# Feed-forward loop: two of eight gate and up tile pairs as 2x2 blocks in seven products

## What is computed

```python
h2 = rms_norm(x, norm2_w[l]) * (1.0 + sc2) + sh2
ff = (jax.nn.silu(h2 @ w_ffn_gate[l]) * (h2 @ w_ffn_up[l])) @ w_ffn_down[l]
x = x + g2 * ff
return rms_norm(x, final_w)
```

## Time and profile before

| | |
|---|---|
| median of three runs | 2235.95 us |
| the profiled execution, first to last instruction | 2234.2 us |
| TensorE busy | 2219.6 us, 99% of the span |
| VectorE / ScalarE / GpSimd busy | 1623.4 / 1104.2 / 136.7 us |
| granted TensorE clock, mean over the span | 0.999 |
| share of TensorE in the chain of work that ended last | 98% |
| HBM traffic | 244 GB/s over the span |

### The profile page before, as it was taken

How to read it: one execution, slowest core, us unless ns; L and a number is a source line. 1 busy time by engine, 2 the same in 40 slices (tenths; PEclk the granted TensorE clock), 3 DMA queues, 4 the chain that set the end, 5 groups by cost and what they waited for, 6 DMA issues and landing times.

```text
span 2234.2 us, 31225 instructions
## 1 busy us (share of the span) xinstructions
PE 2219.6 (99%) x10287; PEld 1848.7 (83%) x10287; DVE 1623.4 (73%) x2120; ACT 1104.2 (49%) x1437; POOL 136.7 (6%) x259
## 2 busy tenths in 40 slices
PE   9999999999999999999999999999999999999998
PEld 7888888888888888888888888888888888888886
DVE  5767778878875875887788877766665666666576
ACT  6455445666664344534366654444444443344444
POOL 1100110000000000010011110000000000000000
PEclk9999999999999999999999999999999999999999
DMA  8978897666665766697689987766766777777664
GB/s 304 339 237 300 314 337 242 208 209 208 214 232 182 288 229 205 211 338 269 197 299 317 325 294 251 243 208 214 235 221 232 238 241 229 237 230 226 209 218 147
DMA packets 157899, 551.78 MB, mean 247 GB/s; under 512 B 19441, under 2 KB 25328, under 8 KB 156288
## 3 DMA queue, kind: packets, MB, share of 16 engines
q1 hardware_dynamic: 112416, 405.92, 53.5%
q0 software_dynamic: 34304, 129.64, 17.0%
q10 hardware_dynamic: 11104, 15.22, 2.0%
HBM read 534.92 MB, written 10.53 MB: 244 GB/s over the span
## 4 chain that ended last, share of the span: by engine, by line
PE 98%; DVE 1%; DMA 1%; ACT 0%; issue 0%; DVEq 0%; ACTq 0%; SPq 0%
PE ps L2090 23%; PE ps L2092 23%; PE ps L2091 23%; PE ps L2208 7%; PE ps L2210 7%; PE ps L2209 7%; PE ps L2129 2%; PE ps L2338 1%; PE ps L2105 1%; PE ps L2107 1%; PE ps L2106 1%; PE ps L2268 0%; PE ps L2333 0%; PE ps L2528 0%; DMA raw<-ws_dram 0%; PE ps L2270 0%
## 5 line engine op out<-in xcount | busy, mean ns | idle before, releaser
L1195 DVE TENSOR_TENSOR w_lo<-raw,w_hi 128x1024 fp32r<-128x1024 f32 x757 | 921.4, 1224 | 512.8 <-ACT w_hi L675 499.1
L675 ACT ACTIVATE w_hi<-raw 128x1024 fp32r<-128x1024 f32 x749 | 788.9, 1060 | 968.6 <-PE ps L2092 818.4
L2090 PE MATMUL ps<-w_hi,a_hi 128*128 128x512 f32 x1612 | 629.6, 391 | 1.1 <-DVE w_lo L1195 1.1
L2092 PE MATMUL ps<-w_hi,a_lo 128*128 128x512 f32 x1612 | 627.8, 389 | 0.0
L2091 PE MATMUL ps<-w_lo,a_hi 128*128 128x512 f32 x1612 | 627.6, 389 | 0.0
L2090 PEld LDWEIGHTS ps<-w_hi,a_hi 128*128 128x128 f32 x1612 | 302.7, 188 | 63.9 <-DVE w_lo L1195 1.5
L2092 PEld LDWEIGHTS ps<-w_hi,a_lo 128*128 128x128 f32 x1612 | 302.7, 188 | 63.0
L2091 PEld LDWEIGHTS ps<-w_lo,a_hi 128*128 128x128 f32 x1612 | 302.8, 188 | 62.1
L2208 PE MATMUL ps<-w_hi,a_hi 128*128 128x512 f32 x640 | 255.6, 399 | 0.0
L2210 PE MATMUL ps<-w_hi,a_lo 128*128 128x512 f32 x640 | 249.9, 391 | 0.0
L2209 PE MATMUL ps<-w_lo,a_hi 128*128 128x512 f32 x640 | 249.4, 390 | 0.0
(11 more groups left out here) (366 smaller groups left out, 2264.7 us busy)
## 6 DMA issues: line engine op xcount, KB each, us to landing
raw<-ws_dram SPq DMA_DIRECT2D x768, 512.0 KB, 4.4
ada<-wa_dram POOLq DMA_DIRECT2D x140, 512.0 KB, 5.0
late<-wa_dram POOLq DMA_DIRECT2D x35, 512.0 KB, 5.5
late_c<-wa_dram POOLq DMA_DIRECT2D x17, 512.0 KB, 5.9
gates_spill<-gst ACTq DMA_DIRECT2D x16, 512.0 KB, 5.3
fT<-fz ACTq DMA_DIRECT2D x160, 32.0 KB, 2.7
ga<-gates_spill POOLq DMA_DIRECT2D x8, 512.0 KB, 4.1
gb<-gates_spill POOLq DMA_DIRECT2D x8, 512.0 KB, 5.5
```

Of the source, the lines that this page charges most:

```text
L675: act.activation(w_hi[:, k.slot(RING), :], raw[:, k.slot(RING), :], ACT.Copy).then_inc(hi_done, 1)
L1195: dve.tensor_tensor(w_lo[:, k.slot(RING), :], raw[:, k.slot(RING), :], w_hi[:, k.slot(RING), :].bitcast(F32), ALU.subtract).then_inc(lo_do ...
L2090: pe.matmul(o, hi(m, tb), w_hi[:, s, cols], start=m == 0, stop=False)
L2092: mm = pe.matmul(o, lo(m, tb), w_hi[:, s, cols], start=False, stop=m == of * kts - 1)
```

## The change

In turns 1 to 9 of the loop the tiles come in the order gate 0, up 0, gate 1, up 1 and so on. Of the eight pairs, pairs 2 and 5 (tiles 4, 5 and tiles 10, 11) are multiplied as 2x2 block matrices: activations by token block and 128-row half, weights by half and by gate or up. Seven block products replace eight (the form with 15 additions), each still of three matmuls, so that such a pair is 21 matmuls: 6 counted to its gate tile and 15 to its up tile.

- The block sums of the activations (`mix_s`, their hi and lo) are made once, in the up tiles of `ff_first` (`act_mix`).
- For each such pair VectorE makes four 128x512 sums of weights (`mixed_sums`), ScalarE rounds them in two instructions of 128x1024 (`split_mixed`), VectorE makes their remainder in one of 128x2048 (`mixed_lo`).
- Three products run into banks 5, 6 and 7 and one into bank 4, over both pairs. ScalarE copies bank 4, VectorE adds the others up (`g_part`, `u_part`), and at the end of the up tiles it adds them to gate and up, before silu and `f_act`.
- The down groups use banks 4 to 7. The pieces of the modulation move from the down groups to behind the splits of tiles 7, 10, 13 and 15. VectorE's two transposes now stand one ahead of and one behind the split of tile 5.
- `rows_turn(3, ...)` moves behind tile 1 of the last chunk, and `rows_copy(3, KT)` behind the 16 DMAs of ScalarE.
- The layout of weights in HBM follows the new order.

```diff
+QUADS = (2, 5)
+MIXED_END = 2 * QUADS[-1] + 2
@@ ScalarE
+            def split_mixed(k, j, n):
+                slot = k.slot(RING)
+                act.wait_ge(raw_landed[slot], k.lap(RING, 16))
+                act.wait_ge(tile_used, (k + (1 - RING)).n)
+                act.activation(w_hi[:, slot, NC:TW], raw[:, slot, NC:TW], ACT.Copy)
...
+                act.wait_ge(w_mix_sum, (sums0 + 2).n)
+                act.activation(mix_hi[:, 0:2], mix_w[:, 0:2], ACT.Copy)
+                act.wait_ge(w_mix_sum, (sums0 + 4).n)
+                act.activation(mix_hi[:, 2:4], mix_w[:, 2:4], ACT.Copy).then_inc(hi_done, 1)
+            def mixed_chunk(k, j):
...
+                step(0)
+                step(1)
+                act.wait_ge(f_lanes, j.n)
+                for b in range(4):
+                    for i in range(4):
+                        act.dma_start(turned[32 * b:32 * b + 32, i], z[32 * i:32 * i + 32, b]).then_inc(f_turned, 16)
+                    step(2 + b)
+                for p in range(6, T_K + 2):
+                    step(p)
+                act_hi(j + -1)
+                for p in range(T_K + 2, 2 * T_K):
+                    step(p)
+                    if p + 1 == MIXED_END:
+                        act.wait_ge(tile_used, (k + MIXED_END).n)
+                        act.activation(g_part[:, 0], ps[:, 4, :], ACT.Copy).then_inc(first_copied, 1)
...
             def ff_chunk(k, g, j):
                 steps(k, 2)
                 steps_sending_f(k + 2, j + -1)
+                rows_copy(3, KT)
                 steps(k + 6, T_K - 6)
...
-            rows_copy(3, KT)
@@ VectorE
+            def mixed_sums(k, j, n, freed):
...
+                dve.wait_ge(hi_done, (k + 1).n)
+                dve.wait_ge(raw_landed[(k + 1).slot(RING)], (k + 1).lap(RING, 16))
+                dve.wait_ge(tile_used, freed.n)
+                dve.tensor_tensor(mix_w[:, 0], u[:, 0:NC], g[:, 0:NC], ALU.subtract).then_inc(w_mix_sum, 1)
+                dve.tensor_tensor(mix_w[:, 1], u[:, NC:TW], u[:, 0:NC], ALU.subtract).then_inc(w_mix_sum, 1)
+                dve.wait_ge(w_mix_sum, (sums0 + 1).n)
+                dve.tensor_tensor(mix_w[:, 2], u[:, NC:TW], mix_w[:, 0], ALU.subtract).then_inc(w_mix_sum, 1)
+                dve.wait_ge(w_mix_sum, (sums0 + 3).n)
+                dve.tensor_tensor(mix_w[:, 3], g[:, NC:TW], mix_w[:, 2], ALU.subtract).then_inc(w_mix_sum, 1)
+                split(k)
+            def mixed_lo(k):
...
+                dve.tensor_tensor(w_lo[:, slot, NC:TW], raw[:, slot, NC:TW], w_hi[:, slot, NC:TW].bitcast(F32), ALU.subtract)
+                dve.tensor_tensor(mix_lo[:], mix_w[:], mix_hi[:].bitcast(F32), ALU.subtract).then_inc(lo_done, 1)
+            def mixed_chunk(k, j, a=None):
...
+                step(0)
+                dve.wait_ge(act_ready, j.n)
+                turning(0)
+                step(1)
+                turning(1).then_inc(f_lanes, 1)
+                step(2)
+                step(3)
+                modulated(0)
+                step(4)
+                step(5)
+                step(6)
+                modulated(1)
+                step(7)
...
@@ TensorE
+                pe.wait_ge(lo_done, (k + 1).n)
+                product(ps[:, 4, :], ah(2 * q, 0), al(2 * q, 0), w_hi[:, g, 0:NC], w_lo[:, g, 0:NC], first, last)
+                product(gate_bank[:, 0], ah(2 * q + 1, 0), al(2 * q + 1, 0), w_hi[:, g, NC:TW], w_lo[:, g, NC:TW])\
+                    .then_inc(tile_used, 1)
+                pe.wait_ge(lo_done, (k + 2).n)
+                product(up_bank[:, 0], mix_s_hi[:, n, 3], mix_s_lo[:, n, 3], w_hi[:, u, NC:TW], w_lo[:, u, NC:TW])
+                product(gate_bank[:, 1], ah(2 * q + 1, 1), al(2 * q + 1, 1), mix_hi[:, 3], mix_lo[:, 3])
+                mixed(ps[:, 5, :], 0, 0, opens=first, closes=last)
+                mixed(ps[:, 7, :], 2, 1, opens=first, closes=last)
+                mixed(ps[:, 6, :], 1, 2, opens=first, closes=last).then_inc(tile_used, 1)
...
+                    for u, bank in enumerate((gate_bank, up_bank)):
+                        if q == 0:
+                            pe.wait_ge(gate_up_free, At(2 * j.base - 1 + u, 2 * j.per, j.i).n)
...
-            rows_turn(3, 5 * KT, 6 * KT)
...
+            for u in range(2):
...
+                    if u == 0 and n == 1:
+                        pe.wait_ge(down_free, 4 * (FC - 1))
+                        rows_turn(3, 5 * KT, 6 * KT)
```

More of the change, by code:

```diff
@@ L894, in _ @@
                 act.sem_inc(a.y_hi_done, 1)
+            for a in (nsa, gqa):
                 act.sem_inc(a.aux_free, 1)
@@ L1130, in _, with step @@
             per = 2 * T_K + 4 * T_Q
+            def split_mixed(k, j, n):
[3 more added lines that the diff above has]
+                act.activation(w_hi[:, slot, NC:TW], raw[:, slot, NC:TW], ACT.Copy)
+                sums0 = At(4 * len(QUADS) * (j.base - 1) + 4 * n, 4 * len(QUADS) * j.per, j.i)
+                act.wait_ge(w_mix_sum, (sums0 + 2).n)
[3 more added lines that the diff above has]
+            def mixed_chunk(k, j):
+                def step(p):
+                    at_ = p + RING
+                    if at_ % 2 and at_ // 2 in QUADS:
+                        split_mixed(k + at_, j, QUADS.index(at_ // 2))
+                    else:
+                        split(k + at_)
+                step(0)
+                step(1)
+                act.wait_ge(f_lanes, j.n)
+                z, turned = (x[:].rearrange("p a t k s -> p a (t k s)") for x in (fz, fT))
+                for b in range(4):
[10 more added lines that the diff above has]
+                        act.activation(g_part[:, 0], ps[:, 4, :], ACT.Copy).then_inc(first_copied, 1)
+                act.wait_ge(act_ready, j.n)
+                act.wait_ge(gate_up_free, At(2 * j.base + 1, 2 * j.per, j.i).n)
+                act.activation(f_silu[:], g_part[:, 0:3:2], ACT.Silu).then_inc(silu_done, 1)
+                for p in range(2 * T_K, per):
+                    step(p)
             def ff_chunk(k, g, j):
@@ L2600, in turn_last, with mixed_quad, product, mixed @@
                         .then_inc(t_done, 1)
[L2602 to L2609, removed]
-                pe.wait_ge(f_split, j.n)
+            def mixed_quad(k, n):
+                q = QUADS[n]
+                g, u = k.slot(RING), (k + 1).slot(RING)
+                first, last = n == 0, n == len(QUADS) - 1
+                def product(out, hi, lo, whi, wlo, opens=False, closes=False):
+                    pe.matmul(out, hi, whi, start=opens, stop=False)
+                    pe.matmul(out, hi, wlo, start=False, stop=False)
+                    return pe.matmul(out, lo, whi, start=False, stop=closes)
+                def mixed(out, s, w, **group):
+                    return product(out, mix_s_hi[:, n, s], mix_s_lo[:, n, s], mix_hi[:, w], mix_lo[:, w], **group)
+                pe.wait_ge(lo_done, (k + 1).n)
[8 more added lines that the diff above has]
+                mixed(ps[:, 6, :], 1, 2, opens=first, closes=last).then_inc(tile_used, 1)
@@ new lines, in mixed_chunk @@
+            def mixed_chunk(k, j):
+                for q in range(T_K):
+                    if q in QUADS:
+                        if q == QUADS[0]:
+                            pe.wait_ge(down_free, At(4 * j.base, 4 * j.per, j.i).n)
+                        mixed_quad(k + 2 * q, QUADS.index(q))
+                        continue
+                    for u, bank in enumerate((gate_bank, up_bank)):
+                        if q == 0:
+                            pe.wait_ge(gate_up_free, At(2 * j.base - 1 + u, 2 * j.per, j.i).n)
+                        tile(k + (2 * q + u), bank, q, T_K, ah, al)
+                pe.wait_ge(f_split, j.n)
+                pe.wait_ge(parts_free, j.n)
+                for c in range(4):
+                    b = 4 + 2 * (c % 2)
+                    if c >= 2:
+                        pe.wait_ge(down_free, At(4 * j.base + c - 1, 4 * j.per, j.i).n)
+                    for n in range(T_Q):
+                        tile(k + (2 * T_K + c * T_Q + n), ps[:, b:b + 2, :], n, T_Q, part(f_hi), part(f_lo))
@@ L2619, in _ @@
-            ff_chunk(k, g, At(FC - 1))
+                mixed_chunk(At(T0["ff"] - per, per, j), At(0, 1, j))
+            k, g = At(T0["ff"] + (FC - 2) * per), At(G0["ff_last"])
+            for u in range(2):
+                pe.wait_ge(gate_up_free, 2 * (FC - 1) - 1 + u)
+                pe.wait_ge(acc_free, (g + (u + 1)).n)
+                for n in range(T_K):
+                    tile(k + (u * T_K + n), pair(g + u), n, T_K, ah, al)
+                    if u == 0 and n == 1:
+                        pe.wait_ge(down_free, 4 * (FC - 1))
+                        rows_turn(3, 5 * KT, 6 * KT)
```

149 lines of the change are left out of this document (113 added, 36 removed).

## The result

The changed kernel takes 2276.84 us (median of 4, 2275.85 to 2277.49), the kernel before 2235.56 beside it: ratio 1.0181, 95% interval 1.0169 to 1.0194. It is slower by 41 us, where 33 were forecast; the time lies inside the range. The profiled execution spans 2274.1 us against 2234.2.

A forecast was written before the change was run, and what follows sets the result against it. TensorE, busy 99% of the span, was taken as the bound. Waits of 45.4 us less 12.2 for 54 fewer matmuls give +33.2: 2267.4 profiled, 2269 us median, range 2252 to 2285.

The forecast's parts named there:

- tile 6, nine turns: TensorE's wait at tile 6 each turn: ready at T+16.9, wanted at T+15.64, a stall of 1.2 us.
- tile 10, nine turns: TensorE's wait at tile 10 each turn: ready at T+28.3, wanted at 27.8, a stall of 0.5 us.
- tile 11: TensorE's wait at tile 11: 2.6 us in turns 1 to 8, behind a modulation piece, and 1.5 in turn 9.
- turn 1, up tile 0: Up tile 0, now second, needs the bank that chunk 0's f_act reads until T+3.66: a 1.0 us wait.
- last chunk, tile 11: Row copy behind 16 DMAs lands late, so tile 11's remainder is late: stall 5.8 us, between 5 and 7.
- last `f_act` late: End of the last chunk: f_act comes about 1 us too late for TensorE's transposes.
- clock: Rival: clock falls behind waits, adding 2.5 us in the last chunk, 12 more if every turn; chance 0.12 together.
- The chain at tile 6: Second transpose ends T+11.9, then four DMA issues 2.44 us, split 1.06, remainder 1.23: tile 6 ready T+16.9.
- The rest of the turn at nothing: Bank 4 copy, PSUM sums and final additions, 4.6 us more VectorE work a turn: cost nothing, other bound 1 us.
- the cost of `act_mix` at nothing: Ahead of the loop, about 4.2 us of VectorE, a remainder and one ScalarE rounding: nothing, or at most 1 us.
- The bounds: DMA issue at 0.55 us takes 10 off, 0.66 adds 8; late raw tiles add 5; hidden last-chunk stall takes 6 off.
- VectorE's room is enough: Rival: VectorE, idle 23.6 of 65 us a turn, absorbs the work; 2223.7, or 2230.5 with last-chunk wait; chance 0.06.

The follow-up runs named there:

- the fastest kernel: Changed kernel with transposes one turn earlier, second modulation piece behind tile 11's remainder, row copy ahead of the last chunk's DMAs: 2224.01 us, ratio 0.9949.
- The single runs: One edit each to the changed kernel: row copy earlier 2270.26 us, both transposes earlier 2251.66, modulation later 2265.13, pair 5 alone as blocks 2241.77.
- transposes ahead: Changed kernel with both of VectorE's transposes ahead of the split of tile 5, same instructions: 2251.66 us, ratio 1.0073.
- the dealt-out issues: Changed kernel with ScalarE's sixteen DMA issues a turn placed two ahead of each of eight splits, not four ahead of four: 2249.35 us, ratio 1.0068.
- two additions: Kernel before with two unused 128x2048 VectorE additions ahead of the first transpose in each of turns 1 to 9: 2261.89 us, ratio 1.0115.
- the one with the row copy ahead: Changed kernel with ScalarE's copy of the turned modulation row ahead of the last chunk's 16 DMAs: 2270.26 us, ratio 1.0159.
- the one with one addition: Kernel before with one unused 128x2048 VectorE addition ahead of the first transpose in each of turns 1 to 9: 2237.66 us, ratio 1.0007.

## Why the prediction was right, and where it was off

Waits of TensorE by place, in us. The measured ones are gaps between starts above 0.2267, the 0.11 of the second matmul with them.

| step | predicted | measured |
|---|---|---|
| tile 6, nine turns | 9 x 1.2 = 10.8 | 1.12 + 7 x 1.55 + 1.74 + 9 x 0.11 = 14.7 |
| tile 10, nine turns | 9 x 0.5 = 4.5 | 9 x (0.41 + 0.11) = 4.7 |
| tile 11 | 8 x 2.6 + 1.5 = 22.3 | 8 x 2.45 + 1.39 + 9 x 0.11 = 22.0 |
| turn 1, up tile 0 | 1.0 | 1.4 |
| last chunk, tile 11 | 5.8 | 4.1 |
| last `f_act` late | 1.0 | 0 |
| clock | 0 (rival: 2.5, or 14.5) | 4.9 |
| sum | 45.4 | 51.8 |

- **What bounds the kernel, and the saving: right.** 54 matmuls at 0.2267; the fastest kernel, in which all but the edge at turn 1 is hidden, returns it.
- **The chain at tile 6: right, its size 0.3 us a turn too small, and 0.1 for the late second matmul.** The second transpose ended at T+12.2 and not T+11.9. The term that failed is the start of the sums: T+4.1 forecast, T+4.44 measured. From the copy of the modulation to the first sum are 0.88 us, 0.71 of them idle; I counted the copy and not the idle time behind it. ScalarE isn't the cause, though the bracket names it: its split of tile 4 ended at T+3.98, as forecast, 0.46 us ahead of the sum. The trace of the kernel before had 0.52 us of idle time behind the same copy (rows below), and I overlooked it. What VectorE does in it stays open. The rest of the chain held to 0.1: tile 6 at T+17.2 for 16.9, tile 10 at T+28.6 for 28.3, tile 11 at T+32.6 for 32.3.

```profile
1815.62 0.16 DVE L2003 COPY mod<-mod_part 128x4 f32 x1
1816.31 1.23 DVE L1195 TENSOR_TENSOR w_lo<-raw,w_hi 128x1024 fp32r<-128x1024 f32 x1 [0.52 <-DVE mod L2003]
```

- **The 128x2048 remainder: right.** 2.28 us, 2.29 forecast from the step between 1024 and 1920 elements.
- **Tiles 10 and 11: right.** The single runs add that their waits are mostly inherited.
- **Turn 1: right mechanism, 0.4 too small.** `f_act` ended at 1552.78 and TensorE started at 1553.06. I left out these 0.28 us of hand-over and the 0.11 of the second matmul.
- **The rest of the turn at nothing, and the cost of `act_mix` at nothing: right.** No line of the table of waits belongs to them.
- **The last chunk: right mechanism, term too large.** From the copy to the landing I took 13.0 us from the earlier trace rows; it was 2195.59 + 7.2 - 2191.60 = 11.2. The load was issued 4.0 us behind the copy, not 5.1, and landed in 7.2, not 7.9. The wait fell below its bounds of 5 to 7.
- **The last `f_act` 1 us late: wrong.** TensorE reaches its transposes at 2226.26 without a gap. With the wait ahead of it shorter by 1.7 us this term of 1.0 had nothing to stand on.
- **The clock: I forecast none in the loop and gave it 0.12 as a rival.** "The granted clock 1.00 in the loop" was one of its signs, and that sign failed. The clock did fall, in the last chunk as the rival had it (1.6 for 2.5 us), and in two turns of nine, where the rival had all nine or none. It is 4.9 of the 6.7 us by which the spans' difference beats the sum. The Trainium skill, "TensorE: Matmul & The Clock Gate", section "Why this matters for your kernels", warns of idle gaps between bursts of matmuls. The trace agrees for the wait of 3.80 us in the last chunk (0.58 behind it). The page speaks of gaps longer than the 2.29 us behind which the clock fell in turns 2 and 6 (0.57 in turn 2), so there the measurement decides; six waits of the same 2.29 us show no fall.
- **The median: 2276.84, forecast 2269.** 6.7 of the 7.8 us are in the span. The other 1.0 is that the profiled execution (2275.85) is the fastest of the four.
- **The sum came closer than its terms.** Without the clock the waits sum to 46.9 us for the 45.4 forecast. But tile 6 was 3.9 too small, tile 10 and turn 1 together 0.6, and the last chunk, the last `f_act` and tile 11 together 3.0 too large; that these nearly cancel is luck.
- **The bounds: of the terms that they name only the last chunk's wait moved, by 1.7 us.** Four issues took 2.44 us as before, and the sums of tile 11 waited for no raw tile in turn 5. One bound is also counted wrong: with 0.55 us an issue, tile 6's 0.24 us are taken twice, and the sum falls by 9 x 0.96 = 8.6 us, not 10. And the 0.07 us until TensorE starts go by an end at 10.44 that the earlier trace rows doesn't give (9.76 + 0.61 is 10.37, which makes 0.14); at tile 6 it was 0.05, so nothing hangs on it.

The rival "VectorE's room is enough" fell for this order of the work and holds for another. It named the right point: the second transpose must end by T+10.7. With an end at T+9.4 (transposes ahead) tile 6 waits no more, at T+12.2 it does. The prediction named the four DMA issues as the term with the widest bound. By its sum, 0.3 us less in each of them would have taken tile 6's wait of 1.2 away; the dealt-out issues show that their place decides it as well.

## What to carry to other kernels

An engine that is idle a third of a turn may still have no room at one place. Measure the margin of the one hand-over that others stand behind, and keep new work off its near side: here 2.2 us more made no wait and the next 2.2 cost 24 us. Before giving up an arithmetic saving, look at what stands in order behind the hand-over (DMA issues on a compute engine's queue, work that nobody waits for soon), since the same instructions in another order turned 41 us of loss into 11 of gain. Where a wait shows at a late tile, look for the first late tile: the wait there may be inherited.

## What the runs showed of the hardware

**The clock falls behind short waits, and not behind each.** With waits of 1.86 us in the bracket (kernel before, two additions) it fell in turns 2, 4, 6 and 8 and not in 3, 5 and 7, and not behind the 2.16 of turn 9. With 2.29 it fell in 2 of 8 turns (turns 2 and 6 of the changed kernel, 1 and 5 of the one with the row copy ahead). The shortest one behind which it fell in these runs had 1.80 (transposes ahead, turn 4); in that run it fell behind 1.84 and 1.91 too and not behind 1.60 to 1.68. Behind the waits of the last chunk, 3.6 to 4.9 us, it fell in all five kernels that have one, for seven to twelve matmuls. Each fall in the loop cost some 1.6 us. In the kernel before, in the one with one addition and in the fastest one it never fell in the loop. I can't say what chooses the turn; no run here was made for that.

**A wait has a price of its own.** 0.16 us of it hide in the row of the matmul ahead, and the second matmul behind it starts 0.11 late.

**An issue of a DMA on ScalarE's queue holds the instruction behind it for about 0.6 us:** 2.44 us for four, 1.16 for two. The Trainium skill, "DMA: Bandwidth & Descriptors", section "Issuing engines are not separate DMA queues", calls the time that the sequencer needs to initiate a DMA usually small relative to the DMA itself. Here it is 0.6 us beside a median of 2.6 from issue to landing, near a quarter, and dealing the issues out gave back two thirds of the loss, because splits stood behind them.
